# An eighth slot in the expert ring, paid for with half of the descriptor scratch; the count vector arrives with the packed constants

## What is computed

```python
q = (tb @ w_q).astype(f32).reshape(blk, PEER_HEADS, 2, half)
s1 = jnp.einsum('thd,hnd->thn', q[:, :, 0], keys1.astype(f32))
s2 = jnp.einsum('thd,hnd->thn', q[:, :, 1], keys2.astype(f32))
v1, i1 = lax.top_k(s1, PEER_TOPK)
v2, i2 = lax.top_k(s2, PEER_TOPK)
...
top_s, top_j = lax.top_k(cand, PEER_TOPK)
expert = jnp.take_along_axis(cand_idx, top_j, axis=-1)
gate = jax.nn.softmax(top_s, axis=-1)
pre = jnp.einsum('thkd,td->thk', u_tab[expert], tb).astype(f32)
act = (jax.nn.gelu(pre) * gate).astype(tb.dtype)
return jnp.einsum('thk,thkd->td', act, v_tab[expert])
```

## Time and profile before

| | before |
|---|---|
| median of 3 runs (lowest, highest) | 3376.12 us (3372.03, 3384.19) |
| the profiled execution, its own time | 3373.29 us |
| its span, first to last instruction | 3371.3 us |
| mean granted TensorE clock | 0.84 |
| PE, DVE, ACT, POOL busy | 81%, 63%, 37%, 36% of the span |
| share of the POOL queue's packets in the time of 16 DMA engines | 81.5% |

### The profile page before, as it was taken

One profiled execution on the slowest core, in us unless ns is written; L12 is line 12 of the kernel. 1 busy time (PEld: TensorE's weight loads), 2 busy tenths in 40 slices (PEclk: granted clock), 3 DMA queues, 4 the chain that ended last, 5 costly groups with the idle time before them and its releaser, 6 DMA issues.

```text
span 3371.3 us, 34626 instructions
## 1 busy us (share of the span) xinstructions
PE 2717.7 (81%) x11134; PEld 1372.6 (41%) x11134; DVE 2109.5 (63%) x4889; ACT 1234.6 (37%) x3752; POOL 1221.1 (36%) x1102
## 2 busy tenths in 40 slices
PE   8789996888988689788977789788788666666777
PEld 7767653444544145344523244344344111111133
DVE  4444688675656786565466785576556776754554
ACT  3211365442333343443333343532333343333332
POOL 0100133553433433334244433343333443433342
PEclk9989997997899689889987799797799676767676
DMA  4205698999999999999999999999999999999998
GB/s 158 75 7 192 232 402 328 392 389 377 411 406 398 391 418 383 383 377 383 413 421 421 393 413 400 376 388 422 378 412 384 390 419 421 376 422 422 421 417 333
DMA packets 186153, 1225.87 MB, mean 364 GB/s; under 512 B 21298, under 2 KB 24130, under 8 KB 50803
## 3 DMA queue, kind: packets, MB, share of 16 engines
q0 software_dynamic: 153024, 1115.00, 81.5%
q1 hardware_dynamic: 32946, 108.66, 8.5%
HBM read 1211.73 MB, written 11.84 MB: 363 GB/s over the span
## 4 chain that ended last, share of the span: by engine, by line
PE 47%; DMA 27%; DVE 15%; ACT 5%; issue 3%; DVEq 2%; POOL 1%; SPq 0%; POOLq 0%; ACTq 0%
PE ps L616 47%; DMA ring<-in_uv,picked 21%; DVE ring L2362 6%; DMA ring<-in_uv,tail_pick 4%; DVEq L2152 1%; ACT scratch L1209 1%; POOL ring L599 1%; ACT gated L1209 1%; ACT diag L1209 1%; DVE scratch L2103 1%; ACT L1209 1%; DMA scratch<-in_keys 1%; ACT act_v L1209 1%; DMA wring<-in_weights 0%; DVE scratch L2107 0%
## 5 line engine op out<-in xcount | busy, mean ns | idle before, releaser
L599 POOL DMA_INDIRECT ring<-in_uv,picked x1024 | 1143.5, 1117 | 1808.3 <-PE ps L616 1712.5
L616 PE MATMUL ps<-ring,diag 128*64 128x512 f32 x4096 | 1345.2, 751 | 490.1 <-ACT diag L1209 486.6
L2362 DVE SCALAR_TENSOR_TENSOR ring<-ring,htok 128x1024 f32<-128x1024 f32 x1024 | 1246.6, 1227 | 702.2 <-DMA ring<-in_uv,picked 697.6
L616 PE MATMUL ps<-hT,wring 128*128 128x256 f32 (+1 forms) x3200 | 797.0, 399 | 18.4 <-DVE hT L1603 8.8
L1209 ACT ACTIVATE act_v<-pre 128x1 f32<-128x1 f32 x1040 | 209.9, 202 | 1555.5 <-DVE ring L2362 1554.5
L616 PEld LDWEIGHTS ps<-ring,diag 128*64 128x64 f32 x4096 | 244.1, 156 | 1197.0 <-ACT diag L1209 1016.0
L616 PEld LDWEIGHTS ps<-hT,wring 128*128 128x128 f32 x3200 | 598.8, 194 | 323.2 <-issue 225.5
L1209 ACT ACTIVATE diag<-folded,gated 128x64 f32<-128x64 f32 x1024 | 356.1, 348 | 33.8 <-PE ps L616 0.4
L1209 ACT ACTIVATE gated<-act_v,gates 128x1 f32<-128x1 f32 x1024 | 301.6, 295 | 33.3
L616 PEld LDWEIGHTS ps<-scratch 128*128 128x128 f32 (+2 forms) x1428 | 207.1, 214 | 152.6 <-issue 89.6
L616 PE MATMUL ps<-scratch 128*128 128x128 f32 (+5 forms) x1428 | 244.2, 317 | 30.0 <-DVE scratch L1750 15.6
(11 more groups left out here) (342 smaller groups left out, 1716.5 us busy)
## 6 DMA issues: line engine op xcount, KB each, us to landing
wring<-in_weights SPq DMA_DIRECT2D x200, 512.0 KB, 7.8
ring<-in_uv,picked POOLq DMA_INDIRECT x1024, 11.8
scratch<-in_keys POOLq DMA_DIRECT2D x4, 1024.0 KB, 10.8
scratch<-in_s_gla POOLq DMA_DIRECT2D x4, 1024.0 KB, 12.3
out_o_gla<-scratch POOLq DMA_DIRECT2D x4, 1024.0 KB, 10.4
scratch<-in_s_dn POOLq DMA_DIRECT2D x1, 2048.0 KB, 12.8
scratch<-in_s_ssm POOLq DMA_DIRECT2D x1, 2048.0 KB, 17.1
out_o_dn<-scratch POOLq DMA_DIRECT2D x1, 2048.0 KB, 11.8
```

What stands on the lines that cost most here:

```text
L599: pool.indirect_dma_start(out=ring[:, g % RING, :], out_offset=None, in_=io["uv"][L], in_offset=bass.IndirectOffsetOnAxis(ap=index, axis=0 ...
L616: return pe.matmul(out, lhsT, rhs, start=start, stop=stop)
L2362: stt(x, x, 1.0, h, MUL, MUL, accum_out=pre[:, g % SMALL:g % SMALL + 1]).then_inc(sem("dotted"), 1)
```

## The change

`RING` is 8. The descriptor scratch is halved to 8192 bytes for each partition, which is what the eighth slot takes. `LAG`, and the slot of the products on `hT`, follow `RING`. The vector 0 to 15 is no longer made on POOL: it stands as 16 more columns in `pack`, and DVE's wait for it at its first top-k is gone.

```diff
-RING = 7
+RING = 8
...
-        iota = sb("iota", [P, TOPK])
...
-        pack = sb("pack", [P, 176])
+        pack = sb("pack", [P, 192])
...
-        row_at, row_at_high = pack[:, 144:160], pack[:, 160:176]
+        row_at, row_at_high, iota = pack[:, 144:160], pack[:, 160:176], pack[:, 176:192]
...
-            pool.iota(iota[:, :], pattern=[[1, TOPK]], base=0, channel_multiplier=0,
-                      allow_small_or_imprecise_dtypes=True).then_inc(sem("iota_ready"), 1)
             front = Strand(mixers())
...
             def choice():
                 for u, (L, t) in enumerate(CHOICES):
-                    if u == 0:
-                        dve.wait_ge(sem("iota_ready"), 1)
...
-    return np.ascontiguousarray(np.concatenate(sides + [r // 8 == j, r % 8 == j, row_at, NKEY * row_at], axis=1)
+    return np.ascontiguousarray(np.concatenate(sides + [r // 8 == j, r % 8 == j, row_at, NKEY * row_at, np.tile(np.arange(TOPK), (P, 1))], axis=1)
...
-    nc = bacc.Bacc("TRN2", target_bir_lowering=False, num_devices=1)
+    nc = bacc.Bacc("TRN2", target_bir_lowering=False, num_devices=1, dynamic_dma_scratch_size=8192)
```

More of the change, by code:

```diff
@@ L2376 @@
     glr_w=(P, KD, 16), head_w=(P, 16), gate2=(17, 512), small_b=(1, 16), a_log=(1, 12),
-    pack=(P, 176), ln_row=(1, D),
+    pack=(P, 192), ln_row=(1, D),
     conv_buf=(P, 3, 20, NS_TOK), s_dn=(P, 32 * P), s_ssm=(P, NS_TOK * 512), s_gla=(P, 32 * 256),
```

## The result

The changed kernel takes 3358.31 us (median of 4 runs, 3352.05 to 3360.97), against 3380.15 us for 4 runs of the kernel before that include the three shown above. The ratio is 0.9943, 95% interval 0.9928 to 0.9959: 0.57% faster, 19 us (0.0057 times 3376), and by the interval 14 to 24 us. The two medians of four runs stand 21.8 us apart, within that. The forecast was 3356 us and a gain of 19.9.

The account below looks back on a forecast made before the run. DMA rate was taken to bound saturated stretches, compute-limited stretches starving DMA between them. Slot -27.3 us plus side DMAs 7.4 gave -19.9, forecast 3356 us from 3376.12; 8 in 10 range 3334 to 3377 us.

Parts of the forecast that it names:

- The bound where DMA is saturated: In saturated stretches gathers come back to back, 2.48 us a pick at 422 GB/s; no ring makes this cheaper.
- The slot: Eighth gather in flight keeps DMA working 2.48 us longer per starving episode; 11 paying episodes give 27.3 us.
- The count of 11: Of 14 episodes with DMA share under 0.90, 11 pay because DVE waits for gathers before the next; three do not.
- fewer windows than 21: Sign to look for: fewer than the 21 windows of 10 us with a DMA share under 0.90.
- DVE's waits for gathers: Sign to look for: DVE's waits for gathers fall below 697.6 us by some 20 to 30 us.
- The side DMAs: Load of s_dn, keys and store of o_gla, behind one more gather in POOL's queue, give back up to 7.4 us.
- The first picks: Gather 7 issues at about 327.8 us, ahead of the products on hT, which still wait for ACT; counted as nothing.
- the scratch: Halved descriptor scratch costs nothing, with estimated room for 56 gathers; POOL's gather issues keep a median near 937 ns.
- the vector: Count vector as 16 more columns, 8 KB in a load DVE needs complete by its first place; counted as nothing.
- The rule against the change: Skill's limit of about 358 GB/s for HBM loads would leave no DMA time to win; the trace's 422 disagrees.
- no change: Rival: PE's backlog follows episodes, so only six with long waits pay; 7.5 us gain, 3369 us; chance 0.26.
- twice as much: Rival: the deeper ring also narrows shallow dips, gaining 51 us, 3325 us; larger gain had chance 0.14.

Follow-up runs that it names:

- run 9: Changed kernel with seven slots and the key, s_dn, s_ssm, s_gla loads and o_gla stores issued from SyncE instead of POOL: 3373.83 us, ratio 0.9995 to the kernel before.
- run 7: Changed kernel, eight slots, lag 8, with key, s_dn, s_ssm, s_gla loads and o_gla stores issued from SyncE instead of POOL: 3339.79 us, ratio 0.9899 to the kernel before.
- run 1: Changed kernel with seven slots again, halved scratch and packed count vector kept: 3378.05 us, ratio 1.0001 to the kernel before.
- run 5: Changed kernel, eight slots, with a descriptor scratch of 2048 bytes in place of 8192: 3351.37 us, ratio 0.9926 to the kernel before.
- run 3: Changed kernel, eight slots, with POOL's side work one gather earlier (lag 7): 3344.90 us, ratio 0.9905 to the kernel before.
- run 8: Changed kernel, eight slots, with a lag of 6 for POOL's side work: 3337.87 us, ratio 0.9886 to the kernel before.
- run 10: Changed kernel, eight slots, with listed side DMAs on SyncE and lag 6 for what stays on POOL: 3344.46 us, ratio 0.9903 to the kernel before.
- run 11: Changed kernel with lag 7 for POOL's side work of layer 1 alone, layer 0 keeping 8: 3350.00 us, ratio 0.9918 to the kernel before.
- run 6: Changed kernel with seven slots and POOL's side work one gather earlier (lag 6): 3374.81 us, ratio 0.9995 to the kernel before.

## Why the prediction was right

The net was met, 19.9 us forecast and 19 measured. The mechanism of both large terms is borne out. The slot's term holds in size within what the runs can tell, and what the side DMAs give back was sized too small.

**The bound where DMA is saturated.** Right: 2.47 us between dots, 422 GB/s, with six slots as with eight.

The traces tell where the slot gained and lost, if the same dot is looked up in each. These are starts of dots in us, numbered from 0 over the 1024 of the prompt:

| dot | before | after | 7 slots, run 9 | 8 slots, run 7 |
|---|---|---|---|---|
| 0 | 374.62 | 377.67 | 379.48 | 374.90 |
| 120 | 744.59 | 746.41 | 750.09 | 742.30 |
| 144 | 822.91 | 824.44 | 829.74 | 819.07 |
| 248 | 1144.33 | 1144.97 | 1153.01 | 1137.41 |
| 256 | 1159.87 | 1158.46 | 1168.62 | 1150.34 |
| 384 | 1540.99 | 1532.93 | 1546.12 | 1525.95 |
| 504 | 1900.25 | 1892.21 | 1905.71 | 1884.92 |
| 512 | 1920.06 | 1908.53 | 1925.76 | 1901.47 |
| 632 | 2270.73 | 2258.42 | 2276.78 | 2251.55 |
| 704 | 2491.27 | 2481.42 | 2491.06 | 2464.87 |
| 712 | 2520.39 | 2516.47 | 2520.60 | 2494.34 |
| 720 | 2547.12 | 2543.20 | 2549.00 | 2522.36 |
| 760 | 2669.17 | 2662.33 | 2670.30 | 2642.08 |
| 768 | 2684.70 | 2674.89 | 2686.49 | 2655.10 |
| 864 | 2935.90 | 2923.42 | 2933.67 | 2901.66 |
| 1023 | 3355.31 | 3343.00 | 3353.51 | 3321.05 |

**The slot, 11 episodes times 2.48 us, 27.3 us.** The mechanism holds. Only the slot counts (run 1). The lead of eight slots over seven grows in steps of about one transfer behind episodes, most cleanly behind those at 1140, 1890 and 2660: 2.1, 3.5 and 3.0 us over the dots 248 to 256, 504 to 512 and 760 to 768, and 2.7, 3.5 and 3.2 between runs 9 and 7. It stands still from 384 to 504 and, in the saturated rest, from 864 on (within 0.6 us). The size is 32 to 34 us by the runs (7 and 9), 25 to 39 by their intervals. In the two traces it is 27.9 from the first dot to the last; the other 4.6 us of their difference lie before the first dot, where no ring plays a part. So 27.3 is not refuted.

The count of 11 is less sure. The episodes do not vanish: 14 before, 15 after. In the windows from 400 to 3330 us 160.9 us of missing DMA time became 148.2, and of these 12.7 us only 4.7 were in windows with a share under 0.90 (73.1 to 68.4). Between runs 9 and 7 it is 9.7 of 25.3, up to 3300 us. The rest lay in the shallower windows, edges of episodes or dips of their own, which the count had left to a rival. I had written that fewer windows than 21 would be under 0.90; there are 20, which shows nothing. And DVE's waits for gathers fell by 107 us where I had written 20 to 30.

**The side DMAs, 3 times 2.48 us, 7.4 us.** The term that was most in error. It was right that a side DMA is there about one gather later, but it left out `s_gla` and the keys of layer 1; the four rows of waits grew by 10.8 us. The three pieces for which I had written 15, 16 and 13 us came to 14.37, 13.76 and 15.27. The table shows where it is lost. From the first dot to the last, eight slots lead by 15.4 us with these DMAs in POOL's queue and by 27.9 without, 12.5 apart. Of these, 9.8 arise from dot 632 to 720, where layer 1's sample states and its last keys are loaded and stored: the change loses 8.4 us there (276.39 to 284.78), 5.9 of them in the eight dots 704 to 712, behind the keys of layer 1, which were not among my three; between runs 9 and 7 it gains 1.4 (272.22 to 270.81). Another 2.6 arise from dot 120 to 144, about `s_dn`, which is little for single executions. The stretch from 632 to 720 repeats well: 276.39 and 277.17 us with seven slots (before, run 1), 284.78 and 281.54 with eight (after, run 5), and 270.71 to 271.28 with eight and either remedy or both (runs 3, 7, 8, 10 and 11). By the runs, the slot's worth there less its net worth is 13 us (32 less 19, both by ratios; its own uncertainty is some 9). The remedies regain 13 us (lag 7), 18.5 (other queue, issued earlier) and 20 (lag 6), each uncertain by 7 to 9.

**The first picks, the scratch, the vector: nothing.** Nothing of them shows: the products on `hT` wait for ACT as before, run 1 holds the rest together at 1.0001, and run 5 shows room at 2048 bytes. The estimate by the Trainium skill, DMA: Bandwidth & Descriptors, The descriptor swizzle, comes to 14 gathers there (2048 / 16 / 9), still above eight and nine; no run went below the point at which it would be short.

**The rule against the change.** By DMA: Bandwidth & Descriptors of the Trainium skill, Where 436 GB/s comes from, loads from HBM stop near 358 GB/s. With nine slots this kernel still gained, and saturated windows hold 422 with six slots as with eight: the trace stands against the 358, and near the port figure of 435.

**The rivals of no change and of twice as much** had 7.5 and 51 us; the interval, 14 to 24 us, leaves out both.

What stays open: why curing the side DMAs is worth nothing beside seven slots (runs 6 and 9, both 0.9995) and 13 to 20 us beside eight. It can't be only the waits themselves, since run 6 shortens them by 8 us, and takes 272.59 us over the dots 632 to 720 against run 1's 277.17, without a gain in the whole. In run 9 the waits for side DMAs are gone but for 1.1 us, and DVE's waits for gathers are 703.6 us against 697.6 before. That fits a picture in which compute, spared those waits, arrives at an empty ring and waits there, and in which an eighth row is what lets it use the time. It was not tested. Nor was the seventh slot's 62 us, which is DMA time that went missing, taken apart by episode.

## What to carry to other kernels

Beside irregular compute, one more slot of this prefetch ring was worth about one transfer time per stretch in which the transfers starved and compute then waited for them. Count such stretches in short windows, not busy shares, and expect more of them for every slot fewer. The longer ring also lengthened the queue that every other DMA of the same issuer stands in: list all of these DMAs that something waits for, not only the first in the chain, and when you lengthen the ring try them earlier in that program, or from another engine. Here a small edit of the lag gave about as much again as the slot did: eight slots with lag 6 take 3337.87 us, against 3358.31 with lag 8. With seven slots the same kind of edit gave nothing (run 6).

## What was not expected of the hardware

The DMA engines held 421 to 422 GB/s of 8 KB rows gathered at random from HBM for 200 us and more at a time, with rings of six, seven and eight slots. And the stores of `o_gla` took 10.2 to 18.7 us to land from POOL's queue in the changed kernel, and 8.3 to 9.1 us from SyncE's in run 7, beside the same gathers.
